# One more expert chunk loaded early: three dense slots for gates and out, and queries, keys and values laid by eight heads

## The reference, cut to what matters

```python
z = einsum('btd,dc->btc', rms_norm(x), w_in)
c_q, c_kv, k_rope, dq, dk, dv, g_mla, g_diff = split(z)      # 256, 256, 32, then five times 1024
q  = norm(c_q) @ w_uq      # 16 heads of 96: 64 plain columns, 32 that are rotated (rope)
kv = norm(c_kv) @ w_ukv    # 16 heads of 64 key and 64 value columns
q, k = head_norm(q), head_norm(concat(k_nope, k_rope))       # then rope on the last 32 columns
o_mla  = softmax(q k^T / sqrt(96)) v                         # 16 heads
o_diff = subln((softmax(q1 k1^T + bias) - lam * softmax(q2 k2^T + bias)) v)   # 8 heads
x = x + (sigmoid(g_mla + b) * o_mla + sigmoid(g_diff + b) * o_diff) @ w_out
h = rms_norm(x); affinity = softmax(h @ router_w)
# 16 experts, each takes its 32 strongest tokens:
x = x + scatter(gate * (silu(xe @ w_gate[e]) * (xe @ w_up[e])) @ w_down[e])   # 24 MB of weights each
# the second block: convolution, stick-breaking attention, spatial gating, MLP, gated projection
```

## Time and profile before

| | |
|---|---|
| median of 3 runs | 1538.57 us |
| profiled execution, its time | 1534.45 us |
| its span, first to last instruction | 1532.0 us |
| PE busy | 1171.6 us (76%) |
| DVE busy | 528.9 us (35%) |
| ACT busy | 378.1 us (25%) |
| POOL busy | 27.2 us (2%) |
| DMA, moved in all | 493.30 MB |
| experts, first matmul to last | 303.16 to 1201.0 us |

### The profile page before, as it was taken

One profiled execution on the slowest core, in us unless ns is written; L12 is line 12 of the kernel. 1 busy time (PEld: TensorE's weight loads), 2 busy tenths in 40 slices (PEclk: granted clock), 3 DMA queues, 4 the chain that ended last, 5 costly groups with the idle time before them and its releaser, 6 DMA issues.

```text
span 1532.0 us, 19837 instructions
## 1 busy us (share of the span) xinstructions
PE 1171.6 (76%) x8197; PEld 693.2 (45%) x8197; DVE 528.9 (35%) x953; ACT 378.1 (25%) x620; POOL 27.2 (2%) x51
## 2 busy tenths in 40 slices
PE   8988788886666666666666666665756899999998
PEld 8766677632122122122121221221221678899887
DVE  6999777511010010110110110110110568666546
ACT  5646645400100000000100100100100364455434
POOL 1000031000000000000000000000000000000000
PEclk9999999997777788777877877878787999999999
DMA  8552222999999999999999999999999763555551
GB/s 295 192 210 93 96 111 99 385 424 427 427 427 426 429 427 428 428 427 427 429 427 427 429 428 427 429 427 429 427 428 428 289 203 103 179 189 185 182 185 53
DMA packets 58615, 493.30 MB, mean 322 GB/s; under 512 B 6666, under 2 KB 8260, under 8 KB 33988
## 3 DMA queue, kind: packets, MB, share of 16 engines
q1 hardware_dynamic: 57620, 491.54, 78.8%
q10 hardware_dynamic: 944, 1.05, 0.2%
HBM read 491.52 MB, written 1.05 MB: 322 GB/s over the span
## 4 chain that ended last, share of the span: by engine, by line
DMA 52%; PE 32%; DVE 12%; ACT 2%; issue 2%; SPq 0%; DVEq 0%; ACTq 0%
DMA arena<-in_expert_w_down 12%; DMA arena<-in_expert_w_up 10%; DMA arena<-in_expert_w_gate 10%; PE ps L1738 9%; PE ps L1829 7%; DMA ring<-in_expert_w_gate 7%; DMA ring<-in_expert_w_up 7%; DMA ring<-in_expert_w_down 7%; PE ps L1743 5%; PE ps L2122 4%; DVE w_split L1055 3%; PE ps L2140 2%; PE ps L1808 1%; DVE stat L1179 1%; PE ps L2199 1%
## 5 line engine op out<-in xcount | busy, mean ns | idle before, releaser
L1055 DVE TENSOR_TENSOR w_split<-ring,w_split 128x1024 fp32r<-128x1024 f32 (+3 forms) x178 | 201.9, 1141 | 107.2 <-ACT w_split L639 106.0
L2122 PE MATMUL ps<-ring,arena 128*32 128x512 f32 x1024 | 165.0, 786 | 92.0 <-DMA ring<-in_expert_w_up 65.5
L2122 PE MATMUL ps<-arena 128*32 128x512 f32 x1024 | 163.7, 782 | 87.2 <-DMA arena<-in_expert_w_up 59.7
L639 ACT ACTIVATE w_split<-ring 128x1024 fp32r<-128x1024 f32 (+3 forms) x178 | 175.2, 990 | 200.5 <-PE ps L1743 143.3
L1474 DVE TENSOR_TENSOR arena<-arena,ps 128x512 f32<-128x512 f32 x16 | 11.0, 687 | 501.1 <-PE ps L2122 501.1
L1481 DVE TENSOR_TENSOR xs<-ps,xs 128x512 f32<-128x512 f32 x64 | 39.7, 683 | 292.6 <-PE ps L2148 292.6
L2122 PEld LDWEIGHTS ps<-ring,arena 128*32 128x32 f32 x1024 | 33.3, 131 | 216.4 <-DMA ring<-in_expert_w_up 107.5
L2122 PEld LDWEIGHTS ps<-arena 128*32 128x32 f32 x1024 | 33.4, 130 | 209.6 <-DMA arena<-in_expert_w_up 96.9
L1829 PE MATMUL ps<-hT_hi,w_split 128*128 128x256 f32 x608 | 111.4, 284 | 0.2 <-DVE arena L1645 0.2
L2140 PE MATMUL ps<-arena 128*32 128x256 f32 x1056 | 83.6, 471 | 32.0 <-DMA arena<-in_expert_w_down 28.3
L2140 PE MATMUL ps<-ring,arena 128*32 128x256 f32 x928 | 74.5, 476 | 41.3 <-DMA ring<-in_expert_w_down 38.4
(11 more groups left out here) (357 smaller groups left out, 1372.8 us busy)
## 6 DMA issues: line engine op xcount, KB each, us to landing
arena<-in_expert_w_gate SPq DMA_DIRECT2D x35, 2048.0 KB, 35.6
ring<-in_expert_w_up SPq DMA_DIRECT2D x35, 2048.0 KB, 36.2
arena<-in_expert_w_up SPq DMA_DIRECT2D x29, 2048.0 KB, 36.4
ring<-in_expert_w_gate SPq DMA_DIRECT2D x29, 2048.0 KB, 36.0
arena<-in_expert_w_down SPq DMA_DIRECT2D x25, 2048.0 KB, 34.5
ring<-in_expert_w_down SPq DMA_DIRECT2D x21, 2048.0 KB, 34.0
ring<-in_w_ff SPq DMA_DIRECT2D x32, 1024.0 KB, 5.0
ring<-in_w_in SPq DMA_DIRECT2D x24, 1024.0 KB, 5.0
```

Source lines behind the costliest of these rows:

```text
L639: act.activation(w_split[:, n % WBUFS, 0, 0:cols], slot_view(slot, cols)[:, n % 2, :], ACT.Copy).then_inc(split_hi, 1)
L1055: dve.tensor_tensor(buf[:, 1, :], w, buf[:, 0, :].bitcast(F32), ALU.subtract).then_inc(split_lo, 1)
L2122: m = pe.matmul(ps[j * CAP:(j + 1) * CAP, bank, :], xe[:, kt, :], w[:, r, j * FCOL:(j + 1) * FCOL], start=kt == 0, stop=kt == KT - 1, skip ...
```

## The change

The dense slots stay five up to the chunks of dv. The twelve chunks of gate_a, gate_b and out go to slots 0, 1 and 4 in turn. Slots 2 and 3 take expert chunk 0 as soon as dv's chunk 18, the last that was there, is split. q, kf and v1 are laid in two groups of eight heads, so that group 0 fills arena place 1 and group 1 arena place 2; PE gives place 1 back in step 11 of the MLA loop, after head 7. SP issues chunk 1 after dense chunk 26 and chunk 2 after dense chunk 30. The release amid out comes after its sixth tile, without a wait for the matmuls, and goes to chunk 6 (slots 0 and 1). DVE does group 0's norm and rope before the MLA loop and group 1's in its steps 1 to 5; the sum of squares and the root move from steps 6 and 7 to 8 and 9.

```diff
-T1_RELEASES = SLOTS - 1
+T1_RELEASES = SLOTS - 2
+LATE_SLOTS = (0, 1, 4)
...
-        q = at(6 * K, HALVES, HEADS * QK)
-        v1 = at(9 * K, HALVES, HEADS * VD)
-        kf = at(11 * K, HALVES, HEADS * QK)
+        GROUPS, IN_GROUP = 2, HEADS // 2
+        attn = at(6 * K, GROUPS, WIDE)
+        q, kf = (attn[:, :, i * 1536:(i + 1) * 1536].rearrange("p g (h c) -> p g h c", h=HALVES) for i in range(2))
+        v1 = attn[:, :, 3072:WIDE].rearrange("p g (h c) -> p g h c", h=HALVES)
...
+        SLOT_OF = [LATE_SLOTS[(i - n_late) % len(LATE_SLOTS)] if n_late <= i < n_first else i % DENSE_SLOTS
+                   for i in range(len(chunks))]
...
-        T1_ORDER = (1, 2, 3, 4, LAST_ARENA, 0, 5, 6, 7, IN_HT)
+        T1_ORDER = (1, 2, 3, 4, LAST_ARENA, 6, 5, 7, IN_HT)
...
-            for i in range(DENSE_SLOTS + 3, n_first):
-                load(i)
-                if i == SPARE_AFTER:
-                    slot, loaded = expert_slot(SPARE)
-                    sp.dma_start(slot, chunk_source(0, SPARE)).then_inc(loaded, 16)
...
+            for i in range(DENSE_SLOTS + 3, n_late + 1):
+                load(i)
+            load_expert(SPARE)
+            load(n_late + 1)
+            sp.wait_ge(split_lo, 2 * (n_late - 1))
+            load_expert(0)
+            for i in range(n_late + 2, n_late + 7):
+                load(i)
+            load_freed(T1_ORDER[0])
+            for i in range(n_late + 7, n_late + 11):
+                load(i)
+            load_freed(T1_ORDER[1])
+            load(n_late + 11)
...
-            step(dve.tensor_tensor(qh, qh, rstd_q.unsqueeze(2).to_broadcast([P, n_heads, QK]), ALU.mult))
-            low_parts("dv", 5, 7)
-            step(dve.tensor_tensor(qh, qh, rows("mla_q_hnorm_w").unsqueeze(1).to_broadcast([P, n_heads, QK]), ALU.mult))
-            low_parts("dv", 7)
+            query_scale(0)
+            low_parts("dv", 5, 6)
+            query_weight(0)
+            low_parts("dv", 6)
...
-                if i == 2:
-                    rope(0)
-                if i == 3:
-                    rope(1)
-                if i == 4:
-                    rope(2)
-                if i == 5 or i == 6:
...
-                if i == 7:
...
+                if 2 <= i < 5:
+                    rope(i - 2, 0)
+                if i == 5:
+                    key_scale(0)
+                if i == 6:
+                    key_rope(0)
...
-                if i == 6:
+                if i == 1:
+                    query_scale(1)
+                if i == 2:
+                    query_weight(1)
+                if i == 3:
+                    rope(0, 1)
+                    rope(1, 1)
+                if i == 4:
+                    rope(2, 1)
+                    key_rope(1)
+                if i == 5:
+                    key_scale(1)
+                if i == 8:
                     dve.wait_ge(od_sums, HALVES)
                     step(dve.tensor_reduce(ss_o, sq.rearrange("p (n d) -> p n d", d=DV), AX, ALU.add))
-                if i == 7:
+                if i == 9:
                     roots(ss_o, rstd_o, 2 * DHEADS, DV, od_root)
...
+                if i == IN_GROUP + 3:
+                    pe.wait_ge(hO_done, DHEADS + IN_GROUP)
+                    pe.sem_inc(chunk_used, 1)
...
-            pe.sem_inc(chunk_used, 2)
+            pe.sem_inc(chunk_used, 1)
...
-            tiles("out", hT, range(0, 2), ready=merge_part)
-            pe.wait_ge(tile_used, TILE0["out"] + 2)
+            tiles("out", hT, range(0, KT - CLOSED["out"]), ready=merge_part)
             pe.sem_inc(chunk_used, 1)
-            tiles("out", hT, range(2, KT - CLOSED["out"]), ready=merge_part)
             closing("out", hT, ready=merge_part, between=lambda: ffn_transposes(0))
             pe.wait_ge(tile_used, done("out"))
-            pe.sem_inc(chunk_used, 3)
+            pe.sem_inc(chunk_used, 2)
```

More of the change, by code:

```diff
@@ L327, in hybrid_blocks @@
                 n_first = len(chunks)
+            if name == "gate_a":
+                n_late = len(chunks)
             TILE0[name], TILES[name], COLS[name], SETS[name] = 2 * len(chunks), rows // P, cols, banks
@@ L337, in slot_view, with earlier @@
             return ring[:, slot, 0:2 * cols].rearrange("p (k c) -> p k c", k=2)
+        SLOT_OF = [LATE_SLOTS[(i - n_late) % len(LATE_SLOTS)] if n_late <= i < n_first else i % DENSE_SLOTS
+                   for i in range(len(chunks))]
+        def earlier(i):
+            return [k for k in range(i) if SLOT_OF[k] == SLOT_OF[i]]
         def landed(i):
-            return 16 * (i // DENSE_SLOTS + 1)
+            return 16 * (len(earlier(i)) + 1)
         ring_f = ring[:, :, :].rearrange("p s n -> p (s n)")
@@ L430, in load @@
             def load(i):
-                slot = i % DENSE_SLOTS
-                if i >= n_first and i - DENSE_SLOTS < n_first:
+                slot, before = SLOT_OF[i], earlier(i)
+                if before and i >= n_first and before[-1] < n_first:
                     sp.wait_ge(chunk_used, dense_freed(slot))
-                elif i >= DENSE_SLOTS:
-                    sp.wait_ge(split_lo, 2 * (i - DENSE_SLOTS + 1))
+                elif before:
+                    sp.wait_ge(split_lo, 2 * (before[-1] + 1))
                 sp.dma_start(slot_view(slot, chunks[i].shape[2]), chunks[i]).then_inc(dense_loaded[slot], 16)
@@ L1201, in rotate, with query_scale @@
                     step(dve.tensor_tensor(x2, x2, t1, ALU.add))
[L1203 to L1208 removed]
+            def query_scale(g):
+                qh = q[:, g].rearrange("p h (n d) -> p (h n) d", d=QK)
+                dve.tensor_tensor(qh, qh, rstd_q[:, g * HEADS:(g + 1) * HEADS].unsqueeze(2).to_broadcast([P, HEADS, QK]),
+                                  ALU.mult).then_inc(dve_step, 1)
+                count[0] += 1
@@ new lines, in query_weight, with rope @@
+            def query_weight(g):
+                qh = q[:, g].rearrange("p h (n d) -> p (h n) d", d=QK)
+                dve.wait_ge(dve_step, count[0])
+                step(dve.tensor_tensor(qh, qh, rows("mla_q_hnorm_w").unsqueeze(1).to_broadcast([P, HEADS, QK]), ALU.mult))
+            def rope(third, g):
+                q4 = q[:, g].rearrange("p h (n d) -> p h n d", d=QK)
+                full = [P, HALVES, IN_GROUP, HR]
+                rotate(q4[:, :, :, NOPE:NOPE + HR], q4[:, :, :, NOPE + HR:QK], cos_t.unsqueeze(2).to_broadcast(full),
+                       sin_t.unsqueeze(2).to_broadcast(full), *[r[:, :, 0:IN_GROUP, :] for r in rope_t], third=third)
```

83 lines of the change are left out of this document (43 added, 40 removed).

## The result

The changed kernel took 1530.19 us (median of 7 runs, 1528.27 to 1532.61), the kernel before 1538.57 in runs beside it (median of 7, 1533.66 to 1542.13). The ratio is 0.9947 with a 95% interval from 0.9929 to 0.9965: faster, by 5.4 to 10.9 us. Forecast were 1533.8 us and 0.9969. Repeated, it gave 1531.13 us and 0.9960 (0.9946 to 0.9973). The prediction had given faster a chance of 0.44 and the same 0.46.

What follows compares the result with a forecast made beforehand. The expert stage was taken as bound by its stream of transfers. Gains 2.0 + 1.5 + 3.3 + 0.4 less cost 2.4 made 4.8 us, giving 1533.8 us, ratio 0.9969; own range 1530.5 to 1537, whole range 1529.5 to 1540.

Steps and rivals of the forecast that it cites:

- Differential attention and dv (1.5 + 3.3): Before the MLA loop: PE's wait for a split in dv goes, 1.5 us; shorter DVE operations in differential attention save 3.3.
- MLA loop (2.4): Group 1's norm and rope come back beside PE in the MLA loop's steps 1 to 5, costing 2.4 us.
- steps 2 and 4: MLA steps with a split, 0.5 us left: the weight costs 1.2 in step 2, rope and key work 1.1 in step 4.
- Step 2's term: MLA step 2, with a split: query weight 1.7 us less the 0.5 left, a cost of 1.2.
- Transfers (2.0): Expert chunks fetched earlier: 181 instead of 185 left, the stream starting at chunk 11's issue after a pause; gain 2.0 us.
- Rival 1: Transfers: no pause before chunk 11, so they give 4.9 instead of 2.0 us, 1530.9 us; chance 0.10.
- part 2: What comes before PE's first expert: time saved there moves chunk 11's issue and the whole stream by the same.
- out (0.4): In out, PE's 0.35 us wait for its own second tile goes: gain 0.4 us.
- POOL and DVE: MLA loop: query weight falls between POOL's two squares; they alternate, and PE loses no more than in the sum.
- Rival 3: MLA loop: moved operations meet POOL's squares, 4.07 us on top of 7.8; 4.7 us slower, 1543.3; chance 0.08.
- Rivals 2 (7.8 us on the path) and 4: 2: group 1's work hidden nowhere, 7.8 instead of 2.4 us, 0.17 with milder forms; 4: dense chunks late, 1543.6, 0.07.
- parts 1 and 2: Part 1: the transfers, gain 2.0 us, from nothing to 4.9; part 2: what comes before PE's first expert.

Runs made afterwards that it cites:

- group 1 back: The changed kernel with group 1's norm and rope done before the MLA loop again; 1536.46 us, ratio 0.9998 to the kernel before.

## Why the prediction was right, and where not

**Differential attention and dv (1.5 + 3.3).** Right. From the query scale to the fourth head the kernel before took 85.88 and 85.95 us in its two profiles, the changed one 81.12: 4.8 us. The clock moves this stretch by about as much: in the repeat and the six variants that leave DVE's order there as it is, it took 79.53 to 83.77 us, in the kernel before with the longer router stage 88.53. It is sharper down to the first head, with 63.28, 63.30 and 63.32 us before and 59.64 to 60.94 after. dv alone, from the query scale to the first scores of the differential attention, went from 11.70 to 10.20. An operation of 256 elements took 0.42 us (reckoned 0.41). 3.6 of the 4.8 had come by the first head, 1.1 came as a shorter wait before gate_b's first tile (1.30 for 2.43). That tile also ran at the higher clock now, 1.6 us faster, and the next step at the lower, 1.6 slower; in the repeat neither was slow, and from the first head to the fourth it took 19.89 us instead of 21.48.

**MLA loop (2.4).** Right in its sum: 2.25 us, by the pair with and without the work. The two waits came at the heads where they were put. What the sum had as 1.2 and 1.1 us for steps 2 and 4 were waits of 0.80 and 0.96; where the other 0.5 us lies stays open. Step 2's term came near its number by luck (see POOL and DVE below).

**Transfers (2.0).** Right: 1.86 us at equal landmarks, the pause in the place forecast, and nothing for the second early chunk (chunk 2 alone moved back). Rival 1, no pause and 4.9 us, is refuted by the share of 0.04. What the working didn't see is the other side of it: with 185 chunks from out's end the router stage had about 2 us of cover, with 181 from chunk 11 it has none. It had a price on part 2 ("moves chunk 11's issue and the whole stream by the same") that holds for the changed kernel only; in the kernel before it is out's end that counts.

**out (0.4).** Right by the wait (0.39), 0.25 us more came with it.

**POOL and DVE.** The query weight met POOL's squares. The timelines of DVE and POOL after:

```profile
186.73 3.45 DVE L1240 TENSOR_TENSOR arena<-arena,row 128x1536 f32<-128x1536 f32 x1
...
191.13 0.82 DVE L1386 TENSOR_SCALAR stat<-stat 128x2 f32<-128x2 f32 x1
```

```profile
186.35 5.58 POOL L617 TENSOR_TENSOR xn<-arena 128x1024 f32<-128x1024 f32 x2 [152.16 <-ACT arena L789]
```

DVE took 3.45 us for what takes 1.75 alone, POOL 5.58 for its pair instead of 4.07: each lost about the length that the other held. The Trainium skill (SBUF — State Buffer, "Who interferes with whom") says that the two shut each other out for the whole instruction; these rows agree. Rival 3 put its price on PE's path, and there most of it was idle time: PE's wait behind it was 0.80 us. It fell because only one of the moved operations meets POOL at all. But the sum had this meeting at nothing, and the rows put the whole 0.80 on it: the maxima that PE's next scores hang on (L1386, the row at 191.13) came 1.70 us later than without POOL by the weight's operation, and 0.65 by their own length (0.82 for 0.17), together more than the wait. Without POOL the weight should have cost PE nothing, an estimate that no run tests, and not the 1.2 us of the sum. The term stood for another wait than the one that came. Rivals 2 (7.8 us on the path) and 4 (no PE wait for weights in gate_b in any profile) didn't come about either.

**Not in the sum.** The end of the MLA loop. From the sixteenth head to the merge the three profiles of the kernel before (that with the longer router stage among them) took 12.28, 12.75 and 12.95 us, those of the changed kernel and its variants 14.40 to 15.59; from the merge to out's first matmul the changed kernel gains back 0.9 to 1.1. The granted clock is at its lower level over some 10 us from 248 us on, while in the kernel before it falls at 255 or later and for 3 to 7 us (stretches above). It goes with the changed kernel and its variants in all eleven profiles. All of them wait 2.29 us instead of 1.93 before the last scores, but for "group 1 back", which waited 1.93 and fell as well. So the wait isn't the cause, or not alone. I name none. The forecast had put nothing here.

**The size.** Counted from the query scale, and down to the last transfer's landing, the changed kernel's profile gains 4.8 before the fourth head, loses 2.0 in the loop and 1.7 at its end, gains 1.1 in the merge, 0.6 in out and 2.3 in the stream: 5.2 us against the second profile of before. Against the first it is 4.8 - 2.2 - 2.1 + 0.9 + 0.6 + 2.0, or 4.0. The forecast of 4.8 lies between them, and that is in part luck: the terms that it had came to 5.2 and 5.8 us, and the loop's end with the merge, which it had not, took 1.2 and 0.6 back.

The medians say 8.4 and, repeated, 5.7 (6.2 by the ratio, 0.9960 of 1538); the second interval, 4.2 to 8.3, takes the sum in, the first, 5.4 to 10.9, doesn't quite. The first median, 1530.19, also lies below the forecast's own range (1530.5 to 1537). It is inside the whole range, 1529.5 to 1540, only because that was widened for rival 1, which the traces refute. And the own range is not what the bounds of parts 1 and 2 add up to: gains of 2.1 to 10.6 us and a cost of 0 to 7.8 give 1528 to 1544.

What else differs between profiles goes with the clock: the start of the program (0 or 1.7 us), the router stage (14.0 or 15.6), the second block (333.0, 334.6 or 336.1 us from the last transfer to the span's end, in steps of 1.5; from 66 to 100 us behind the last expert's sum the granted clock is 0.92 in the second profile of before and 1.00 in the first). The kernel before has two of its three profiles at 336.1 to 336.2, the changed one and its variants one of eleven (336.1; the run with chunks 0 and 2 moved back, whose last landing isn't to be read, took as long as the first profile of the changed kernel from the last expert's sum on, 330.49 us). Whether that is the kernel's doing or a small sample is open. So the forecast erred by 3.6 us in the time (by 1.4 on the repeat's ratio), and the experiments don't put that on a term of the sum.

## What to carry to other kernels

Ask what starts the last unbroken stream and count from there: a change that moves that point uncovers work that had cover (here the router stage). Put moved work into one step that is idle throughout rather than a piece into each of several that are nearly full; in the loop that took away 2.25 us, though the time didn't show it. Before a row of big transfers is made unbroken, look for the small transfer on another queue that is wanted soon after.

## What the runs showed of the hardware

The same transfer of 256 KB on ACT's queue took 16 us from issue to landing beside three chunks of 2 MB on SP's queue, 24 us beside five, and 34 us in a row of nine: its time went with what was under way beside it. A DVE operation over 1536 elements took 1.75 us alone and 3.45 us beside POOL's multiplications, and POOL's pair 5.58 instead of 4.07. And stretches at TensorE's lower clock come and go between executions of the same kernel, so that one landmark moves by 1.6 us: the same instruction started at 107.06 and at 105.46 us.
